# Forgetting attention: mask and key decay added by TensorE, maxima and exponentials taken from the bank

## The chip, the cores and the metric

The kernel runs on one core of one Trainium2 chip. The metric is the device time of one execution in microseconds; of several runs the median is taken. The program covers a whole two-block model plus a mixture-of-experts layer, and the part that is changed is one stage of it, some 45 us long.

## The reference, cut to what matters

All of it is float32, 256 tokens, model width 1024. The second block is "forgetting attention" with 16 heads of 64:

```
log_f = log_sigmoid(f + b_f)                       # one value per token and head
cum   = cumsum(log_f, axis=tokens)                 # per head
for each block of 128 queries (qs .. qe):
    logits = q[qs:qe] @ k[:qe].T + cum[qs:qe, None] - cum[None, :qe]
    p      = softmax(where(query >= key, logits, -inf))
    out    = p @ v[:qe]
```

A softmax over keys doesn't change when a value is added to a whole row, so `cum` of the query (one value for each row) has no effect on `p`; `cum` of the key has.

## The kernel before, in words

Everything is written out by hand: one program for each engine, and semaphores between them. Matmul results go to eight PSUM banks that are handed out in the fixed order of a list (`bank_plan`, line 210 and on for this stage). Each entry of the list names a product and the engine that empties its bank ("A" for ScalarE, "D" for VectorE). `take_bank` on TensorE waits until the bank taken eight entries earlier has been emptied; `bank_filled` counts the filled ones, `emptied["A"]` and `emptied["D"]` count the emptied ones of each engine in the order of the list.

The queries and keys are laid out with the head's 64 values on partitions (`fqT`, `fkT`). A head has two tiles of scores in one bank: queries 0 to 127 against keys 0 to 127 (128 columns), queries 128 to 255 against all keys (256 columns). The stage is a loop over 16 heads, skewed across the engines:

- TensorE, step i (lines 1004 to 1014): the scores of head i (`fox_scores`), the turning of the probabilities of head i-2 (`fox_turn`, three 128x128 transposes, line 991), and in every even step from 4 on the product with the values for a pair of heads (`fox_read`, lines 1001 and 1002). The scores are four float32 matmuls: for each of the two tiles the product of query and key (L982), then a product that adds the key's decay row (L984): a one-hot column of the identity, broadcast, picks the head's row out of `ncumT`.
- VectorE, step i (lines 1846 to 1873): adds the query's decay (`cum`) and the mask to both tiles, bank to SBUF (L1852, L1854; after this the bank is free), takes the negated row maxima from SBUF (L1858, L1859), then for head i-1 the reciprocal of the row sums and the scaling of the probabilities (L1864 to L1866), and in every even step from 4 on the gating of a finished pair (L1871, L1872, L1563).
- ScalarE, step i (lines 1345 to 1356): the two exponentials with row sums (L1348, L1350), then the copy of the turned probabilities of head i-2 out of their bank (L1356).

`logits`, `prob` and `mx` have two buffers. VectorE starts head i after the exponentials of head i-2 are done.

Ahead of the loop TensorE computes the decay sums by six small matmuls into bank `fox_cum` (L965 to L970), and then transposes queries (`fox_qT`) and keys (`fox_kT`) into four banks each (L780). `transpose_in` takes its four banks before its first transpose. In the list stand `fox_cum`, four `fox_qT`, four `fox_kT`: the last bank of the keys is the one that `fox_cum` had, eight entries earlier. VectorE copies `cum` and builds `ncumT` (L1839 to L1841), then copies the keys out (L1843). ScalarE scales the queries (L1340). After the loop comes the output product of the stage (`out_product`, L768 to L770).

SyncE loads weights into a ring of three slots; a slot is loaded again when its old weights have been split into `units` by ScalarE and VectorE. `fp32r` in the rows is the rounded float32 type; large products use it, in three matmuls of high and low parts.

Of the kernel before, what the change touches and what calls it, by code (L numbers as in the profile page):

```python
# [33 lines left out]
F32 = mybir.dt.float32  # L34
I32 = mybir.dt.int32
ACT = mybir.ActivationFunctionType
ALU = mybir.AluOpType
AX = mybir.AxisListType

P = 128  # L40
# [147 lines left out]
def bank_plan():  # L188

    def total(layer, j):  # L190
        return [("mod_sum", SUMS.index((layer, j)), "D")] + ([("mod_sum_high", layer, "D")] if j == GATE else [])

    g = [("c_cols", 0, "A"), ("vecs", 0, "D")] + [("x0T", i, "A") for i in range(4)] + total(0, SCALE) + total(0, SHIFT)
    g += [("ret_q", i, "D") for i in range(RH)]
    g += [("ret_k", i, "D") for i in range(RH)]
    g += [("ret_v", i, "A") for i in range(6)] + total(0, GATE) + [("ret_v", i, "A") for i in range(6, 8)]
    g += [("ret_g", i, "A") for i in range(2)] + total(1, SCALE) + [("ret_g", i, "A") for i in range(2, 4)]
    g += [("ret_s", h, "D") for h in range(2)]
    g += [("ret_g", i, "A") for i in range(4, 6)] + total(1, SHIFT) + [("ret_s", h, "D") for h in range(2, RH)]
    g += [("ret_o", i, "D") for i in range(4)]  # L200
    g += [("ret_g", i, "A") for i in range(6, 8)]
    g += [("ret_o", i, "D") for i in range(4, 8)]
    g += [("ret_uT", i, "S") for i in range(8)]
    g += [("ret_y", i, "D") for i in range(4)]
    g += [("x1T", i, "A") for i in range(4)]
    g += [("fox_q", 0, "D"), ("fox_q", 1, "D"), ("fox_f", 0, "D"), ("fox_q", 2, "D"), ("fox_q", 3, "D")]
    g += total(1, GATE) + [("fox_k", i, "D") for i in range(4)]
    g += [("fox_v", i, "A") for i in range(4)] + [("fox_g", i, "A") for i in range(4)]
    g += [("fox_cum", 0, "D")]
    g += [("fox_qT", i, "A") for i in range(4)] + [("fox_kT", i, "D") for i in range(4)]  # L210
    for i in range(FH + 3):
        if i < FH:
            g += [("fox_s", i, "D")]
        if 2 <= i < FH + 2:
            g += [("fox_pT", i - 2, "A")]
        if i >= 4 and i % 2 == 0:
            g += [("fox_o", (i - 4) // 2, "D")]
    g += [("fox_y", i, "D") for i in range(4)]
    g += [("x2T", i, "S") for i in range(4)]
    for c in range(2):  # L220
        g += [("conf_g", 2 * c + i, "A") for i in range(2)] + [("conf_a", 2 * c + i, "D") for i in range(2)]
    g += [("conf_taps", i, "A") for i in CONV_BY_TENSOR]
    g += [("conf_cT", i, "D") for i in range(4)] + [("conf_nT", i, "A") for i in range(4)]
    g += [("conf_y", i, "D") for i in range(4)]
    g += [("x3T", i, "S") for i in range(4)]
    for c in range(6):
        n = min(2, FB // 2 - 2 * c)
        g += [("ffn_gate", 2 * c + i, "A") for i in range(n)] + [("ffn_up", 2 * c + i, "D") for i in range(n)]
    g += [("ffn_y", i, "D") for i in range(4)]
    g += [("x4T", i, "S") for i in range(4)]  # L230
    for c in range(2):
        g += [("sc_c", 2 * c + i, "A") for i in range(2)] + [("sc_h", 2 * c + i, "D") for i in range(2)]
        g += [("sc_b", 2 * c + i, "D") for i in range(2)]
    g += [("sc_y", i, "D") for i in range(4)]
    g += [("x5T", i, "A") for i in range(4)]
    g += [("route", 0, "D"), ("rank", 0, "D")]
    return g
# [58 lines left out]
def build(nc, t, out):  # L296
# [4 lines left out]
    with ctx:  # L301
        def sb(name, shape, dt=F32):
            return ctx.enter_context(nc.sbuf_tensor(name, shape, dt))
# [10 lines left out]
        xr_at = nc.sbuf_base  # L314
        xr = sb("xr", [P, 2, KB, T], F32R)
        X = nc.alloc_sbuf_tensor_at("X", [P, (KB + 1) * T], F32, offset=xr_at)
        region_at = nc.sbuf_base
        R = nc.alloc_sbuf_tensor_at("R", [P, REGION], F32, offset=region_at)
        H = nc.alloc_sbuf_tensor_at("H", [P, REGION], F32R, offset=region_at)
# [11 lines left out]
        bf_row = sb("bf_row", [P, FH])  # L331
        logf = sb("logf", [P, NT, FH])
        logf_t = sb("logf_t", [P, 2, NT * FH])
        cum = sb("cum", [P, NT, FH])
        mx = sb("mx", [P, 2, 2])
        rsum = sb("rsum", [P, 2, 2])
        rinv = sb("rinv", [P, 2, 2])
# [55 lines left out]
        y_tmp = region(10240, 2, 512)  # L393
        wf = region(7424, KB, FH)

        ncumT = X[:, 0:T]
        xn1 = region(8192, NT, D)
        fq_tok, fk_tok = region(0, NT, D), region(2048, NT, D)
        fv, fgT = region(4096, NT, D), region(6144, KB, T)
# [2 lines left out]
        fqT = [region(8192, KB, T), X[:, T:T + KB * T].rearrange("p (k t) -> p k t", k=KB)]  # L402
        fuT = split_region(0, KB, T)
        fsq = region(12288, 2, 512)
        logits = region(12288, 2, 384)
        prob = region(13056, 2, 384)
        probT = region(13824, 4, 384)

# [83 lines left out]
        logf_mid = sem("logf_mid")  # L492
        logf_ready = sem("logf_ready")
        logits_ready = sem("logits_ready")
        probs_exp = sem("probs_exp")
        probs_ready = sem("probs_ready")
        half_ready = sem("half_ready")
        conv_ready = sem("conv_ready")
# [247 lines left out]
        def _(pe):  # L746
# [215 lines left out]

            pe.wait_ge(logf_ready, 1)
            b = take_bank("fox_cum", 0)
            mm(b[:, 0:FH], tri, logf[:, 0, :], start=True, stop=True)  # L965
            mm(b[:, FH:2 * FH], ones, logf[:, 0, :], start=True, stop=False)
            mm(b[:, FH:2 * FH], tri, logf[:, 1, :], start=False, stop=True)
            mm(b[0:FH, P:2 * P], logf[:, 0, :], tri, start=True, stop=True)
            mm(b[0:FH, 2 * P:3 * P], logf[:, 0, :], ones, start=True, stop=False)
            mm(b[0:FH, 2 * P:3 * P], logf[:, 1, :], tri, start=False, stop=True).then_inc(bank_filled, 1)  # L970
            wait_emptied("fox_q", 3)
            transpose_in("fox_qT", fq_tok)
            wait_emptied("fox_k", 3)
# [2 lines left out]
            def fox_scores(h):  # L976

                b = take_bank("fox_s", h)
                blk = h // 2
                pick = ident[:, h:h + 1].to_broadcast([P, P])  # L980
                for tt, lo, n in ((0, 0, P), (1, P, T)):
                    mm(b[:, lo:lo + n], fqT[h % 2][:, blk, tt * P:(tt + 1) * P], fkT[:, blk, 0:n],  # L982
                       start=True, stop=False)
                    last = mm(b[:, lo:lo + n], pick, ncumT[:, 0:n], start=False, stop=True)  # L984
                last.then_inc(bank_filled, 1)

            def fox_turn(h):
# [205 lines left out]
        def _(act):  # L1193
# [149 lines left out]
            for i in range(FH + 2):  # L1343
                if i < FH:
                    act.wait_ge(logits_ready, i + 1)
                    if i >= 2:
                        act.wait_ge(bank_filled, BANK_AT["fox_pT", i - 2] + 1)
                    nc.scalar.activation(prob[:, i % 2, 0:P], logits[:, i % 2, 0:P], ACT.Exp,  # L1348
                                         bias=mx[:, i % 2, 0:1], accum_out=rsum[:, i % 2, 0:1])
                    nc.scalar.activation(prob[:, i % 2, P:3 * P], logits[:, i % 2, P:3 * P], ACT.Exp,  # L1350
                                         bias=mx[:, i % 2, 1:2], accum_out=rsum[:, i % 2, 1:2]).then_inc(probs_exp, 1)
                if i >= 2:
                    h = i - 2
                    if h >= 4:
                        act.wait_ge(bank_filled, BANK_AT["fox_o", (h - 4) // 2] + 1)
                    nc.scalar.copy(probT[:, h % 4, :], bank("fox_pT", h)[:, 0:3 * P]).then_inc(emptied["A"], 1)  # L1356
# [182 lines left out]
        def _(dve):  # L1539
# [296 lines left out]
            for key in (("fox_v", 0), ("fox_v", 1), ("fox_g", 0)):  # L1836
                lows_until(CHUNK_AT[key] + 2)
            b = bank("fox_cum", 0)
            v.tensor_copy(cum[:, :, :].rearrange("p t h -> p (t h)"), b[:, 0:NT * FH])  # L1839
            step(v.memset(ncumT, 0.0))  # L1840
            v.tensor_scalar(ncumT[0:FH, :], b[0:FH, P:3 * P], -1.0, None, ALU.mult).then_inc(emptied["D"], 1)  # L1841
            for g in range(4):
                v.tensor_copy(fkT[:, 2 * g:2 * g + 2, :], pairs(bank("fox_kT", g))).then_inc(emptied["D"], 1)  # L1843

            wait_emptied("fox_kT", 3)
            for i in range(FH + 3):
                if i < FH:
                    b = bank("fox_s", i)
                    if i >= 2:
                        dve.wait_ge(probs_exp, i - 1)  # L1850
                    j = i % 2
                    v.scalar_tensor_tensor(logits[:, j, 0:P], b[:, 0:P], cum[:, 0, i:i + 1],  # L1852
                                           const[:, C_MASK + P:C_MASK + 2 * P], ALU.add, ALU.add)
                    v.scalar_tensor_tensor(logits[:, j, P:3 * P], b[:, P:3 * P], cum[:, 1, i:i + 1],  # L1854
                                           const[:, C_MASK:C_MASK + 2 * P], ALU.add, ALU.add
                                           ).then_inc(emptied["D"], 1)
                    wait_emptied("fox_s", i)
                    v.tensor_reduce(mx[:, j, 0:1], logits[:, j, 0:P], AX.X, ALU.max, negate=True)  # L1858
                    v.tensor_reduce(mx[:, j, 1:2], logits[:, j, P:3 * P], AX.X, ALU.max, negate=True  # L1859
                                    ).then_inc(logits_ready, 1)  # L1860
                if 1 <= i <= FH:
                    h, j = i - 1, (i - 1) % 2
                    dve.wait_ge(probs_exp, h + 1)
                    step(v.reciprocal(rinv[:, j, :], rsum[:, j, :]))  # L1864
                    v.tensor_scalar(prob[:, j, 0:P], prob[:, j, 0:P], rinv[:, j, 0:1], None, ALU.mult)
                    v.tensor_scalar(prob[:, j, P:3 * P], prob[:, j, P:3 * P], rinv[:, j, 1:2], None, ALU.mult  # L1866
# [370 lines left out]
```

## Time and profile before

| what | value |
| --- | --- |
| median of 3 runs | 1893.32 us (1892.92 to 1893.88) |
| profiled execution, its own time | 1889.13 us |
| span of the profiled execution | 1887.2 us |
| mean granted TensorE clock | 0.973 |
| PE busy | 1747.1 us (93%) |
| DVE busy | 1424.1 us (75%) |
| ACT busy | 1020.0 us (54%) |

How to read it: the span goes from the first to the last instruction; busy time is the sum over an engine's instructions without overlaps. PE is TensorE, PEld its weight loads, DVE VectorE, ACT ScalarE, SP SyncE. A duration contains the time in which the next instruction of the same engine is already in the pipe, so the distance between two starts is often shorter than the duration. A float32 matmul stands as two records ("x2"), an fp32r matmul as one.

### The profile page before, as it was taken

The numbers are of one execution on the slowest core, as the hardware profiler recorded it, in microseconds if no ns is written. First come the engines' busy times: TensorE is split into PE (matmuls) and PEld (weight loads), VectorE is DVE, ScalarE is ACT, GpSimd is POOL, SyncE is SP. The second block draws the span as 40 slices with busy tenths as digits, with TensorE's granted clock in tenths as the row PEclk, the third lists the DMA queues.
The fourth block names the chain that finished last, engine by engine and source line by source line (L and its number), as shares of the span: only waits on it lengthen the run. The fifth ranks groups of instructions, "written<-read, shape, count | busy, mean of one in ns | idle before, by whom it ended". The sixth has DMA issues, their size and how long they took to land.

```text
span 1887.2 us, 23377 instructions
## 1 busy us (share of the span) xinstructions
PE 1747.1 (93%) x9401; PEld 1487.6 (79%) x9401; DVE 1424.1 (75%) x1253; ACT 1020.0 (54%) x804; POOL 52.0 (3%) x42
## 2 busy tenths in 40 slices
PE   2899889988989999797999999999999999999995
PEld 2888678967769998796788887888878888888784
DVE  5686866485865553576787987988979799898896
ACT  1334244454224332332776777767777677677762
POOL 0000002000000000001000000000000000000100
PEclk9999899999999999897999999999999999999998
DMA  9579173604655656453999999999999999999992
GB/s 336 190 288 361 68 256 137 219 3 148 180 182 201 246 195 230 156 179 123 336 361 370 382 372 368 368 371 380 371 374 365 374 387 372 386 382 383 370 379 112
DMA packets 217700, 531.19 MB, mean 281 GB/s; under 512 B 7606, under 2 KB 13902, under 8 KB 217337
## 3 DMA queue, kind: packets, MB, share of 16 engines
q1 hardware_dynamic: 210624, 514.52, 74.8%
q10 hardware_dynamic: 5640, 10.39, 1.5%
q0 software_dynamic: 1328, 4.73, 0.7%
q8 instruction: 82, 1.34, 0.3%
q14 instruction: 26, 0.21, 0.0%
HBM read 521.93 MB, written 16.09 MB: 285 GB/s over the span
## 4 chain that ended last, share of the span: by engine, by line
PE 79%; DVE 9%; DMA 5%; ACT 3%; issue 2%; POOL 1%; ACTq 0%; DVEq 0%; POOLq 0%; SPq 0%
PE psum L768 25%; PE psum L770 25%; PE psum L769 25%; DMA ring<-in_moe_w_gate 3%; DVE units L1563 3%; DMA ring<-in_moe_w_up 1%; ACT units L1445 1%; PE psum L1129 1%; DMA ring<-in_mod_w 1%; POOL root_out L1512 1%; DVE R L1910 1%; DVE stats L1973 1%; DMA R<-in_positions 0%; DVE R L1637 0%; DVE x L1982 0%
## 5 line engine op out<-in xcount | busy, mean ns | idle before, releaser
L1563 DVE TENSOR_TENSOR units<-ring,units 128x2048 fp32r<-128x2048 f32 x451 | 1011.0, 2279 | 271.2 <-ACT units L1243 167.6
L1445 ACT CAST units<-ring 128x2048 fp32r<-128x2048 f32 x332 | 625.5, 1916 | 237.1 <-PE psum L770 69.9
L768 PE MATMUL psum<-units,xr 128*128 128x512 f32 x1120 | 445.2, 397 | 13.4 <-DVE units L1563 6.0
L770 PE MATMUL psum<-units,xr 128*128 128x512 f32 x1120 | 438.9, 392 | 0.0
L769 PE MATMUL psum<-units,xr 128*128 128x512 f32 x1120 | 438.6, 392 | 0.0
L1243 ACT CAST units<-ring 128x2048 fp32r<-128x2048 f32 (+1 forms) x119 | 218.8, 1882 | 219.3 <-PE psum L770 186.3
L768 PE MATMUL psum<-units,H 128*128 128x512 f32 x696 | 274.6, 395 | 2.1 <-DVE H L1563 2.1
L769 PE MATMUL psum<-units,H 128*128 128x512 f32 x696 | 272.4, 391 | 0.0
L770 PE MATMUL psum<-units,H 128*128 128x512 f32 x696 | 272.2, 391 | 0.0
L768 PEld LDWEIGHTS psum<-units,xr 128*128 128x128 f32 x1120 | 211.8, 189 | 61.0 <-issue 9.3
L768 PE MATMUL psum<-xr,units 128*128 128x256 f32 x864 | 247.1, 286 | 12.6 <-DVE units L1563 11.4
L770 PEld LDWEIGHTS psum<-units,xr 128*128 128x128 f32 x1120 | 211.7, 189 | 45.3
L769 PE MATMUL psum<-xr,units 128*128 128x256 f32 x864 | 246.5, 285 | 0.0
L770 PE MATMUL psum<-xr,units 128*128 128x256 f32 x864 | 246.4, 285 | 0.0
L769 PEld LDWEIGHTS psum<-units,xr 128*128 128x128 f32 x1120 | 212.0, 189 | 43.4 <-issue 0.7
L768 PEld LDWEIGHTS psum<-xr,units 128*128 128x128 f32 x864 | 168.1, 195 | 13.6 <-DVE units L1563 11.4
L769 PEld LDWEIGHTS psum<-xr,units 128*128 128x128 f32 x864 | 168.0, 194 | 0.0
L770 PEld LDWEIGHTS psum<-xr,units 128*128 128x128 f32 x864 | 167.9, 194 | 0.0
L768 PEld LDWEIGHTS psum<-units,H 128*128 128x128 f32 x696 | 131.6, 189 | 30.2 <-issue 1.8
L770 PEld LDWEIGHTS psum<-units,H 128*128 128x128 f32 x696 | 131.5, 189 | 27.9
L769 PEld LDWEIGHTS psum<-units,H 128*128 128x128 f32 x696 | 131.7, 189 | 26.9
L2146 DVE TENSOR_TENSOR R<-R,psum 128x512 f32<-128x512 f32 x56 | 38.4, 685 | 33.4 <-PE psum L770 33.4
(260 smaller groups left out, 1022.1 us busy)
## 6 DMA issues: line engine op xcount, KB each, us to landing
ring<-in_moe_w_gate SPq DMA_DIRECT2D x56, 2048.0 KB, 9.7
ring<-in_moe_w_up SPq DMA_DIRECT2D x56, 2048.0 KB, 10.2
ring<-in_moe_w_down SPq DMA_DIRECT2D x56, 2048.0 KB, 9.8
ring<-in_mod_w SPq DMA_DIRECT2D x12, 2048.0 KB, 9.8
ring<-in_ret_w_in SPq DMA_DIRECT2D x11, 2048.0 KB, 9.7
ring<-in_fox_w_in SPq DMA_DIRECT2D x8, 2048.0 KB, 8.9
ring<-in_sc_w_in SPq DMA_DIRECT2D x6, 2048.0 KB, 7.9
ring<-in_ffn_w_gate SPq DMA_DIRECT2D x5, 2048.0 KB, 8.4
```

The lines of the kernel that those rows point to most:

```text
L768: mm(dst, left[0], right[0], start=first, stop=False)
L769: mm(dst, left[0], right[1], start=False, stop=False)
L770: return mm(dst, left[1], right[0], start=False, stop=last)
L1129: last = nc.tensor.transpose(b[:, j * P:(j + 1) * P], e_ht[:, (q * PAIRS + c) % 2, j * P:(j + 1) * P], ident)
L1243: nc.scalar.copy(dst[0], src).then_inc(unit_high, 3 - len(parts))
L1445: nc.scalar.copy(*expert_unit_parts(q, j, half, 0)).then_inc(unit_high, 1)
L1512: nc.gpsimd.tensor_tensor(root_out[:, n % 2, 0:w], root_in[:, n % 2, 0:w], neg_half[:, 0:w], ALU.pow).then_inc(root_ready, 1)
L1563: return v.tensor_tensor(dst, src, high.bitcast(F32), ALU.subtract)
L1910: ins = v.scalar_tensor_tensor(conv[:, i, :], u_pad[:, i, k:k + T], vec[:, i, V_DW + k:V_DW + k + 1], conv[:, i, :], ALU.mult, ALU.add)
L1973: last = v.bn_stats(stats[:, tt, half, :], z[:, tt, hs])
L2146: v.tensor_tensor(e_ht[:, (q * PAIRS + c) % 2, :], e_s[:, (q * PAIRS + c) % 2, :], psum[:, 4 + (q * 2 * PAIRS + 2 * c + 1) % 4, :], ALU.mu ...
```

## The change

The query's decay is no longer added. The mask and the key's decay are both added by TensorE, in fp32r: two matmuls of 384 columns ahead of the two score products take the place of the two float32 decay matmuls. So that nothing of the decay is lost to rounding, it is held as a rounded part (partitions 0 to 15) and the remainder (partitions 32 to 47), and the one-hot column has a one for each. VectorE takes the maxima from the bank, ScalarE the exponentials; the exponentials now empty the bank. The tiles `logits` and `cum` go, and the semaphore `probs_exp` with them: its waits are on the emptied bank now.

```diff
-            g += [("fox_s", i, "D")]
+            g += [("fox_s", i, "A")]
...
-            mm(b[:, 0:FH], tri, logf[:, 0, :], start=True, stop=True)
-            mm(b[:, FH:2 * FH], ones, logf[:, 0, :], start=True, stop=False)
-            mm(b[:, FH:2 * FH], tri, logf[:, 1, :], start=False, stop=True)
-            mm(b[0:FH, P:2 * P], logf[:, 0, :], tri, start=True, stop=True)
-            mm(b[0:FH, 2 * P:3 * P], logf[:, 0, :], ones, start=True, stop=False)
-            mm(b[0:FH, 2 * P:3 * P], logf[:, 1, :], tri, start=False, stop=True).then_inc(bank_filled, 1)
+            for at in (0, QUAD):
+                rows_at = b[at:at + FH]
+                mm(rows_at[:, P:2 * P], logf[:, 0, :], tri, start=True, stop=True)
+                mm(rows_at[:, 2 * P:3 * P], logf[:, 0, :], ones, start=True, stop=False)
+                last = mm(rows_at[:, 2 * P:3 * P], logf[:, 1, :], tri, start=False, stop=True)
+            last.then_inc(bank_filled, 1)
...
-                pick = ident[:, h:h + 1].to_broadcast([P, P])
+                pick = pick_r[:, h:h + 1].to_broadcast([P, P])
+                mm(b[:, 0:3 * P], ident_r, mask_r, start=True, stop=False)
+                mm(b[:, 0:3 * P], pick, ncum, start=False, stop=False)
                 for tt, lo, n in ((0, 0, P), (1, P, T)):
-                    mm(b[:, lo:lo + n], fqT[h % 2][:, blk, tt * P:(tt + 1) * P], fkT[:, blk, 0:n],
-                       start=True, stop=False)
-                    last = mm(b[:, lo:lo + n], pick, ncumT[:, 0:n], start=False, stop=True)
+                    last = mm(b[:, lo:lo + n], fqT[h % 2][:, blk, tt * P:(tt + 1) * P], fkT[:, blk, 0:n],
+                              start=False, stop=(tt == 1))
...
-                    nc.scalar.activation(prob[:, i % 2, 0:P], logits[:, i % 2, 0:P], ACT.Exp,
+                    b = bank("fox_s", i)
+                    nc.scalar.activation(prob[:, i % 2, 0:P], b[:, 0:P], ACT.Exp,
                                          bias=mx[:, i % 2, 0:1], accum_out=rsum[:, i % 2, 0:1])
-                    nc.scalar.activation(prob[:, i % 2, P:3 * P], logits[:, i % 2, P:3 * P], ACT.Exp,
-                                         bias=mx[:, i % 2, 1:2], accum_out=rsum[:, i % 2, 1:2]).then_inc(probs_exp, 1)
+                    nc.scalar.activation(prob[:, i % 2, P:3 * P], b[:, P:3 * P], ACT.Exp,
+                                         bias=mx[:, i % 2, 1:2], accum_out=rsum[:, i % 2, 1:2]).then_inc(emptied["A"], 1)
...
-            v.tensor_copy(cum[:, :, :].rearrange("p t h -> p (t h)"), b[:, 0:NT * FH])
-            step(v.memset(ncumT, 0.0))
-            v.tensor_scalar(ncumT[0:FH, :], b[0:FH, P:3 * P], -1.0, None, ALU.mult).then_inc(emptied["D"], 1)
+            v.tensor_copy(mask_r[:, 0:P], const[:, C_MASK + P:C_MASK + 2 * P])
+            v.tensor_copy(mask_r[:, P:3 * P], const[:, C_MASK:C_MASK + 2 * P])
+            v.tensor_copy(ident_r, ident)
+            v.tensor_tensor(pick_r, ident[:, 0:FH], ident[:, QUAD:QUAD + FH], ALU.add)
+            step(v.memset(ncum.bitcast(F32), 0.0))
+            step(v.tensor_scalar(ncum_high[QUAD:QUAD + FH, :], b[QUAD:QUAD + FH, P:3 * P], -1.0, None, ALU.mult))
+            for lo, n in ((0, P), (P, T)):
+                v.tensor_scalar(ncum[0:FH, lo:lo + n], b[0:FH, P:P + n], -1.0, None, ALU.mult)
+                last = v.scalar_tensor_tensor(ncum[QUAD:QUAD + FH, lo:lo + n], b[QUAD:QUAD + FH, P:P + n], -1.0,
+                                              ncum_high[QUAD:QUAD + FH, 0:n].bitcast(F32), ALU.mult, ALU.subtract)
+            last.then_inc(emptied["D"], 1)
...
-            wait_emptied("fox_kT", 3)
             for i in range(FH + 3):
                 if i < FH:
                     b = bank("fox_s", i)
                     if i >= 2:
-                        dve.wait_ge(probs_exp, i - 1)
+                        wait_emptied("fox_s", i - 2)
                     j = i % 2
-                    v.scalar_tensor_tensor(logits[:, j, 0:P], b[:, 0:P], cum[:, 0, i:i + 1],
-                                           const[:, C_MASK + P:C_MASK + 2 * P], ALU.add, ALU.add)
-                    v.scalar_tensor_tensor(logits[:, j, P:3 * P], b[:, P:3 * P], cum[:, 1, i:i + 1],
-                                           const[:, C_MASK:C_MASK + 2 * P], ALU.add, ALU.add
-                                           ).then_inc(emptied["D"], 1)
-                    wait_emptied("fox_s", i)
-                    v.tensor_reduce(mx[:, j, 0:1], logits[:, j, 0:P], AX.X, ALU.max, negate=True)
-                    v.tensor_reduce(mx[:, j, 1:2], logits[:, j, P:3 * P], AX.X, ALU.max, negate=True
+                    v.tensor_reduce(mx[:, j, 0:1], b[:, 0:P], AX.X, ALU.max, negate=True)
+                    v.tensor_reduce(mx[:, j, 1:2], b[:, P:3 * P], AX.X, ALU.max, negate=True
                                     ).then_inc(logits_ready, 1)
                 if 1 <= i <= FH:
                     h, j = i - 1, (i - 1) % 2
-                    dve.wait_ge(probs_exp, h + 1)
+                    wait_emptied("fox_s", h)
```

The new tiles `ncum`, `ncum_high`, `mask_r`, `ident_r` and `pick_r` lie in the memory of `xr`, which is free in this stage.

## Rows read from the trace of the kernel before

**Rows 1.** Windows view: length; busy of PE, PEld, DVE, ACT, POOL; PEclk; DMA share; GB/s.

```profile
403.36:408.70 5.34, 4.54 (x32) 3.51 (x31) 4.91 (x18) 2.70 (x10) 0.00 (x0) 1.00 0.01 3
```

**Rows 2.** Timeline by engine, the same pair; columns: start, duration, engine, line; idle before.

```profile
403.36 0.35 DVE L1852 SCALAR_TENSOR_TENSOR R<-psum,cum,const 128x128 f32<-128x128 f32 x1 [0.22 <-PE psum L984]
404.13 0.29 DVE L1858 TENSOR_REDUCE mx<-R 128x1 f32<-128x128 f32 x1
...
404.78 0.40 ACT L1348 ACTIVATE R<-R,mx 128x128 f32<-128x128 f32 x1 [2.03 <-DVE mx L1859]
...
406.27 0.66 PE L1001 MATMUL psum<-R 128*64 128x256 f32 x4 [0.21 <-ACT R L1356]
407.08 0.49 PE L982 MATMUL psum<-R,X 128*128 128x128 f32 x2
407.41 0.39 PE L984 MATMUL psum<-X,const 128*128 128x128 f32 x2
407.63 0.60 PE L982 MATMUL psum<-R,X 128*128 128x256 f32 x2
408.06 0.59 PE L984 MATMUL psum<-X,const 128*128 128x256 f32 x2
408.50 0.49 PE L991 MATMUL psum<-const,R 128*128 128x128 f32 x3
...
408.70 0.35 DVE L1852 SCALAR_TENSOR_TENSOR R<-psum,cum,const 128x128 f32<-128x128 f32 x1 [0.22 <-PE psum L984]
```

**Rows 3.** Timeline, TensorE and VectorE at the end of the loop.

```profile
424.37 0.66 PE L1001 MATMUL psum<-R 128*64 128x256 f32 x4 [0.71 <-ACT R L1356]
...
425.29 0.42 DVE L1871 TENSOR_TENSOR R<-psum,R 128x256 f32<-128x256 f32 x1 [0.86 <-PE psum L1002]
...
426.42 2.29 DVE L1563 TENSOR_TENSOR units<-ring,units 128x2048 fp32r<-128x2048 f32 x1
```

**Rows 4.** Groups by line and shape: reads of PSUM beside reads of SBUF.

```profile
L1563 DVE TENSOR_TENSOR H<-R,H 128x256 fp32r<-128x256 f32 x8 | 3.4, 425 | 0.3
L1871 DVE TENSOR_TENSOR R<-psum,R 128x256 f32<-128x256 f32 x8 | 3.4, 419 | 1.5 <-PE psum L1002 1.5
L1350 ACT ACTIVATE R<-R,mx 128x256 f32<-128x256 f32 x16 | 7.9, 495 | 0.0
L1372 ACT ACTIVATE R<-psum,vec 128x256 f32<-128x256 f32 x6 | 2.9, 475 | 21.5 <-PE psum L1030 21.5
```

**Rows 5.** Chain of waits: one fp32r matmul of 512 and one of 256 columns.

```profile
425.91 0.23 PE psum L770
...
456.03 0.12 PE psum L769
```

**Rows 6.** Timeline, ahead of the loop and its first heads, three engines.

```profile
376.14 3.71 PE L780 MATMUL psum<-const,R 128*128 128x128 f32 x32
376.25 0.19 DVE L1839 COPY cum<-psum 128x32 f32<-128x32 f32 x1 [5.94 <-PE psum L970]
376.44 0.27 DVE L1840 MEMSET X<- 128x256 f32 x1
376.75 0.41 DVE L1841 TENSOR_SCALAR X<-psum 16x256 f32<-16x256 f32 x1
379.24 2.48 DVE L1843 COPY R<-psum 128x512 f32<-128x512 f32 x4 [2.08 <-PE psum L780]
...
382.25 1.28 ACT L1348 ACT_TABLE_LOAD   x1
...
385.82 0.39 PE L982 MATMUL psum<-R,X 128*128 128x128 f32 x2
...
388.76 0.40 ACT L1348 ACTIVATE R<-R,mx 128x128 f32<-128x128 f32 x1 [0.76 <-DVE mx L1859]
```

**Rows 7.** Waits of the load queue from 360 to 440 us; columns: total, times, longest.

```profile
SPq L678 <- DVE units L1563: 71.3, 2, 60.2
```

**Rows 8.** Windows view, a stretch with a lower granted clock.

```profile
220.00:240.00 20.00, 17.26 (x65) 14.03 (x66) 19.68 (x21) 1.65 (x3) 0.00 (x0) 0.76 0.38 126
```

More of the change, by code:

```diff
@@ L316, in build @@
         X = nc.alloc_sbuf_tensor_at("X", [P, (KB + 1) * T], F32, offset=xr_at)
+        Xr = nc.alloc_sbuf_tensor_at("Xr", [P, 2 * KB * T], F32R, offset=xr_at)
         region_at = nc.sbuf_base
@@ L333, in build @@
         logf_t = sb("logf_t", [P, 2, NT * FH])
-        cum = sb("cum", [P, NT, FH])
         mx = sb("mx", [P, 2, 2])
@@ L394, in build @@
         wf = region(7424, KB, FH)
-        ncumT = X[:, 0:T]
+        ncum = Xr[:, KB * T + T:KB * T + T + 3 * P]
+        ncum_high = Xr[:, KB * T + T + 3 * P:KB * T + T + 3 * P + T]
+        mask_r = Xr[:, 3072:3072 + 3 * P]
+        ident_r = Xr[:, 3456:3456 + P]
+        pick_r = Xr[:, 3584:3584 + FH]
         xn1 = region(8192, NT, D)
@@ L404, in build @@
         fsq = region(12288, 2, 512)
-        logits = region(12288, 2, 384)
         prob = region(13056, 2, 384)
@@ L494, in build @@
         logits_ready = sem("logits_ready")
-        probs_exp = sem("probs_exp")
         probs_ready = sem("probs_ready")
```

## The prediction

> **What bounds the kernel now.** I read the page first (its slices show TensorE nearly always busy and the load engines silent in one slice only, that of the attention loop), then the windows over that loop, the chain of waits through it, the timeline of each engine over one pair of heads, and the groups by shape for the prices. The reader is to see that this stage, unlike most others, is not held by any one engine's work. A pair of heads takes 5.34 us, in which TensorE is busy 4.54, VectorE 4.91 and ScalarE 2.70 [rows 1]. What repeats is a ring of waits through all three [rows 2]: VectorE adds and reduces, from 403.36 to the exponential at 404.78, 1.42; exponentials and copy of the turned probabilities until TensorE reads them at 406.27, 1.49; that product until the next scores start at 407.08, 0.81; scores until VectorE starts at 408.70, 1.62. The sum is 5.34, the whole period. So what the change cuts from this ring counts in full, once for each pair, until another ring takes over.
>
> **The scores (L982, L984).** Removed: two float32 decay matmuls, 408.06 to 408.50 and 407.41 to 407.63, 0.44 + 0.22 = 0.66 [rows 2]. Added: two fp32r matmuls of 384 columns. 256 columns take 0.12, 512 take 0.23 [rows 5], so one takes between these; I take the middle, 0.175, so 0.35 for both (0.24 to 0.46). Net -0.31 a head; a ring has one head's scores in it. Scores after a read go from 1.62 to 1.31.
>
> **VectorE in the loop.** L1852 and L1854 go, and with them the wait for their own end: from 403.36 to the first maximum at 404.13, 0.77 a head [rows 2]. The maxima read PSUM instead of SBUF. No row has a reduction from PSUM; the nearest pair is the tensor_tensor, 419 ns from PSUM against 425 from SBUF [rows 4], so I take no difference; the two maxima until the exponential stay at 404.13 to 404.78, 0.65. Ceiling: that they take as long as the two removed passes over the same columns, 0.77, or 0.12 more; the other end is a gain of 0.01.
>
> **ScalarE in the loop.** Same instructions, from PSUM. With a per-partition operand, 256 columns take 475 ns from PSUM and 495 from SBUF [rows 4] (the latter writes row sums too). I take 0; from 0.04 less to 0.04 more a head.
> On these two the Trainium skill speaks against half of the change: "VectorE: DVE Perf Modes", section on the TRN2 errata, gives VectorE 58 fixed cycles from SBUF and 120 from PSUM, and ScalarE 224 and 172. By that, as an estimate, two maxima cost 0.13 more and two exponentials 0.09 less, 0.04 more a ring, about 0.3 in all; the VectorE rows above don't show the difference.
>
> **New period.** 0.65 + 1.49 + 0.81 + 1.31 = 4.26, so 1.08 less. What is late next: the route from the read over the gating of the finished pair: read at 424.37 to the gate at 425.29, 0.92, gate to the next instruction at 426.42, 1.13 [rows 3], then 0.65 + 1.49: 4.19. Just below 4.26, so it hides, but more savings on TensorE would be lost to it. By work, TensorE would be busy 4.54 - 0.62 = 3.92, VectorE 4.91 - 1.54 = 3.37 [rows 1], so neither is the bound. VectorE's second head of the pair and its waits for the exponentials of the head before fit: they end at most 0.65 + 1.49 after its maxima began, and the scaling of that head comes only after the other head's scaling and maxima. The bank of head i is freed by the exponentials instead of the first passes, some 2 us later; it is wanted three heads on, over 6 us later: nothing.
>
> **Ahead of the loop.** TensorE: three 128-wide small matmuls out, three more 16-wide in, all of a kind with the transposes, 3.71 over 32 = 0.116 a record [rows 6]; 0, within 0.2.
> VectorE: before, three instructions, 376.25 to about 377.16 [rows 6]. Now ten, all behind the wait for the `fox_cum` bank: mask copies, identity and pick about 0.8, memset of 384 columns with its wait 0.45 (256 take 0.31 from start to start), the rounded row 0.46 with its wait (0.41 for the like), then 0.3 + 0.4 + 0.45 + 0.5 for the four that fill `ncum`: 3.3 in all (2.0 if each takes 0.2, 4.6 if each takes 0.46). They end at 379.55.
> Who waits: `transpose_in` for the keys takes its four banks first, and the last of them is `fox_cum`'s. Before, that bank was free at 377.16 and the query transposes ended at 376.14 + 16 x 0.116 = 378.00, so it cost nothing. Now the key transposes start at 379.6, 1.6 late (0.3 to 2.9), so key copies start at 379.24 + 1.6 = 380.84, take 2.48, and the first maxima are done at 383.32 + 0.65 = 383.97. The cover is ScalarE's table load, 382.25 to 383.53, behind which the first exponential stood anyway. What sticks out is 0.44 (0 to 1.75).
>
> **The sum.** Through the first heads: the scores of head 3 start at 385.82 [rows 6], behind the turn of head 0, which follows from exponential 0, so now at 386.26. Behind a turn they took 0.1 less than behind a read (first distance 0.22 instead of 0.33), so 1.21 now: maxima at 387.47, exponential 3 at 388.12 instead of 388.76 [rows 6]: 0.64 won. From there to exponential 15 are six rings (scores of heads 5, 7, ... 15): 6 x 1.08 = 6.48. The tail behind exponential 15 (read of pair 6, turn 15, copy, read of pair 7) has no changed length. Won at the start of the output product: 7.1 us.
>
> **Behind the loop.** The load queue sleeps through the stage: it waits 71.3 us for VectorE's split of weights, 60.2 in one piece [rows 7], the DMA share in the loop is 0.01 [rows 1]. The ring is full before the loop starts, so nothing that runs on its own clock is overtaken; loads, splits and products move forward together. The saving should reach the end whole.
> The profiled execution took 1889.13 us (span 1887.2), so 1882.0 by its own measure. The median of the runs shown is 4.2 above it; the difference is applied to that: 1893.3 - 7.1 = 1886.2.
>
> **Rivals.**
> Smaller gain: reductions from PSUM at their ceiling (6 x 0.12 = 0.7), fp32r matmuls at 0.23 each (6 x 0.11 = 0.7) and the setup at its own (1.3) leave 4.4: 1888.9. For it: no row shows these forms. Against it: each nearest row is better. 0.14.
> The mask product isn't cheap: an fp32r matmul joined to float32 ones in one accumulation runs at their rate. 384 columns are then 0.44 x 1.5 = 0.66 each, two of them 1.3 instead of 0.66: period 5.22 rather than 5.34, and 6 x 0.12 is about what the setup loses: 1893, no change. Against it: rate goes with an instruction's own type in all rows. 0.04.
> The gain doesn't travel: some later stage starts at a time set by loads. Then 1893.3. For it: the expert layer keeps the DMA engines full. Against it: rows 7; its loads too start only when slots come free. 0.06.
> Slower: the chip grants TensorE the lower of its two levels, 1.2 instead of 2.4 GHz, in this loop. It is 1.00 there now [rows 1], and 0.76 in a stretch where the engine is busy by the record 17.26 of 20 us [rows 8], so a fall is possible at such shares. Then the 3.92 us of matmuls in a pair become some 7.2 and TensorE itself the bound: 1.9 more than now for each of 7 pairs, +13, 1906. From about a third of the loop at the lower level on, the gain is eaten. Against it: the same products in less time, 3.92 of 4.26, a busier engine than 4.54 of 5.34. The Trainium skill ("TensorE: Matmul & The Clock Gate", "What's actually happening") says that activity releases the throttle, which speaks against this rival as well. 0.04.
>
> **Chances and range.** Forecast 0.72, the rest as above. What this kernel's measurement tells from no change is 0.2%, 3.8 us. Faster 0.72 + 0.14 = 0.86; within 0.2% 0.10; slower 0.04. The low end takes the good bounds (no setup cost, 0.12 matmuls: 8.3 won, and half a us for the runs), 1884.4; the high end takes the smaller gain whole and 0.6 for the runs, 1889.5. That leaves out 0.14 for the other three rivals and a little at each end.
>
> **What would show it.** Right: VectorE's maxima of odd heads 4.26 apart; the first key copy at about 380.8 instead of 379.24; the first exponential at about 384.0; the key transposes in a group of their own, waiting for VectorE; the last read of a pair at about 417.3 instead of 424.37; the stretches behind it unchanged in length. Wrong: a period above 4.6, a reduction from PSUM above 0.5 us, a granted clock below 1.00 in the loop, or a longer idle of TensorE for loads further on.

## The result, and the profile after

| | before | changed |
| --- | --- | --- |
| first timing, median of 7 | 1893.32 us | 1881.79 us |
| ratio, 95% interval | | 0.9947 (0.9936 to 0.9958) |
| profiled execution, span | 1889.13, 1887.2 us | 1882.47, 1880.7 us |

The kernel is faster, and by more than was forecast: the median lies 2.6 us below the range. Two later timings of the same kernel gave 0.9966 (0.9950 to 0.9982) and 0.9959 (0.9943 to 0.9974). Read the profile first for the part that was changed.

One pair of heads in the loop, in the windows view (length; busy PE, PEld, DVE, ACT, POOL; clock; DMA), the answer to [rows 1]:

```profile
402.61:406.81 4.20, 3.93 (x28) 3.00 (x27) 3.62 (x14) 2.57 (x10) 0.00 (x0) 1.00 0.01 4
```

And the ring of waits in the timeline, the answer to [rows 2] and to the gating of [rows 3]:

```profile
404.70 0.66 PE L1004 MATMUL psum<-R 128*64 128x256 f32 x4
405.50 0.44 PE L983 MATMUL psum<-Xr 128*128 128x384 f32 x1
405.78 0.34 PE L984 MATMUL psum<-Xr 128*128 128x384 f32 x1
405.96 0.82 PE L986 MATMUL psum<-R,X 128*128 128x128 f32 x4
406.61 0.49 PE L994 MATMUL psum<-const,R 128*128 128x128 f32 x3
...
405.61 0.42 DVE L1876 TENSOR_TENSOR R<-psum,R 128x256 f32<-128x256 f32 x1 [0.39 <-PE psum L1005]
406.07 0.29 DVE L1877 CAST H<-R 128x256 fp32r<-128x256 f32 x1
406.40 0.43 DVE L1567 TENSOR_TENSOR H<-R,H 128x256 fp32r<-128x256 f32 x1
406.81 0.29 DVE L1863 TENSOR_REDUCE mx<-psum 128x1 f32<-128x128 f32 x1
...
407.47 0.37 ACT L1352 ACTIVATE R<-psum,mx 128x128 f32<-128x128 f32 x1 [1.54 <-DVE mx L1864]
...
408.90 0.66 PE L1004 MATMUL psum<-R 128*64 128x256 f32 x4
```

The period is 4.20 instead of 5.34. "Read" is the product with the values for a pair of heads (L1004 here). Two routes lead from the read at 404.70 to the maxima at 406.81, and they arrive together. On one, the scores end when the next turn (L994) starts, 406.61, and some 0.2 later VectorE could go on. On the other, the gating starts at 405.61 and holds VectorE for 1.20. Then the maxima take 0.66, and exponentials and copy 1.43 until the next read at 408.90.

The groups by shape, the answer to [rows 4]: maxima from SBUF in the kernel before, then maxima and exponentials from PSUM in the changed one.

```profile
L1859 DVE TENSOR_REDUCE mx<-R 128x1 f32<-128x256 f32 x16 | 6.5, 409 | 0.0
...
L1864 DVE TENSOR_REDUCE mx<-psum 128x1 f32<-128x256 f32 x16 | 6.6, 413 | 0.0
L1354 ACT ACTIVATE R<-psum,mx 128x256 f32<-128x256 f32 x16 | 7.4, 466 | 0.0
```

Ahead of the loop, the answer to [rows 6]: the transposes stand in two groups now, and the keys' wait for VectorE's setup.

```profile
374.44 1.97 PE L782 MATMUL psum<-const,R 128*128 128x128 f32 x16
377.67 1.94 PE L782 MATMUL psum<-const,R 128*128 128x128 f32 x16 [1.26 <-DVE Xr L1851]
...
374.55 0.23 DVE L1843 CAST Xr<-const 128x128 fp32r<-128x128 f32 x1 [5.60 <-PE psum L971]
...
377.11 0.42 DVE L1851 SCALAR_TENSOR_TENSOR Xr<-psum,Xr 16x256 fp32r<-16x256 f32 x1
378.99 2.48 DVE L1855 COPY R<-psum 128x512 f32<-128x512 f32 x4 [1.47 <-PE psum L782]
...
381.11 1.28 ACT L1352 ACT_TABLE_LOAD   x1 [0.57 <-PE psum L986]
...
386.46 0.37 ACT L1352 ACTIVATE R<-psum,mx 128x128 f32<-128x128 f32 x1 [0.32 <-DVE mx L1864]
```

The end of the loop:

```profile
415.17 0.66 PE L1004 MATMUL psum<-R 128*64 128x256 f32 x4 [0.71 <-ACT R L1360]
```

S is the length of the stage from the first query transpose to this last read. It is 415.17 - 374.44 = 40.73; before, 424.37 - 376.14 = 48.23 [rows 3, 6]. So the change took 7.5 us out of the stage. The first timing shows 11.5. The experiments ask what the ring of waits is made of, and where the other 4 us are.

### The profile page after: what moved, and what is told of

It is laid out like the page before. It is cut to its first block, busy times and chain, and to the rows that moved or that the text cites. A ratio compares the mean times of both kernels' runs of the same rounds, so it can differ in the third digit from the quotient of the medians.

```text
span 1880.7 us, 23289 instructions
## 1 busy us (share of the span) xinstructions
PE 1739.5 (92%) x9369; PEld 1481.5 (79%) x9369; DVE 1414.6 (75%) x1228; ACT 1017.5 (54%) x804; POOL 51.4 (3%) x42
## 4 chain that ended last, share of the span: by engine, by line
PE 66%; DVE 6%; DMA 3%; issue 2%; ACT 2%; POOL 1%; SPq 0%; POOLq 0%; DVEq 0%; ACTq 0%
PE psum L770 21%; PE psum L772 20%; PE psum L771 20%; DVE units L1567 2%; DMA ring<-in_moe_w_gate 1%; PE psum L1132 1%; DMA ring<-in_moe_w_up 1%; ACT units L1449 1%; POOL root_out L1516 1%; DVE stats L1978 1%; DVE x L1987 0%; DVE R L1915 0%; PE psum L986 0%; DMA u_rows<-R 0%; DVE R L1975 0%
```

## The experiments

**Is the further gain the change's?** The changed kernel again, the changed kernel with the unused tile `cum` put back, the kernel before with `cum` moved behind the other small tiles, and later the changed kernel once more.

> The changed kernel once more. S is the stage from the first query transpose to the last read of a pair: 48.2 us before, 40.7 after the change. Theory R (the ring is all of it): S is again 40.7 and the kernel is 7.5 us faster than before within the spread of the runs; the further 4 us of the first timing were spread. Theory L (the removed tile moved every small tile behind it by 128 bytes, and that brought more): 11 to 12 us faster again. Theory D (later stages run faster because they come at another time): 11 to 12 again as well, and a stage behind the loop is shorter in this profile too.

> The changed kernel with the unused tile cum still allocated, so that all tiles behind it lie where they lay before. Theory L: 4 us of the gain are lost, about 1886. Theories R and D: as the repeat of the changed kernel beside it, within 1 us.

```diff
+        cum = sb("cum", [P, NT, FH])
         mx = sb("mx", [P, 2, 2])
```

> The kernel before with cum allocated last, so that the tiles behind it lie as in the changed kernel. Theory L: 4 us faster than before. Theories R and D: no change, S 48.2.

```diff
-        cum = sb("cum", [P, NT, FH])
...
         gate_back = sb("gate_back", [P, 2, NT])
+        cum = sb("cum", [P, NT, FH])
```

> The changed kernel a third time, in the same rounds as the version beside it. By the ring alone S is 40.7 again and the time 7.5 us below before. If the first timing (11.5 below) was the true size, it is 11 to 12 below; in this profile the length of the expert layer, 986 to 995 us in the profiles so far, decides where its own time falls, not S.

Measured: the repeat 0.9966, the padded one 0.9960 (0.9942 to 0.9978), the moved `cum` 1.0007 (0.9995 to 1.0019), the last repeat 0.9959. The layout (theory L) falls: neither kernel moved by 4 us. What these timings did show is how far runs of one kernel lie apart: 34 runs of before span 1885.05 to 1897.85, twelve of the changed kernel 1876.12 to 1892.11.

Every kernel's profile can be cut into four stretches: up to the first query transpose; S; from there to VectorE's last step for the router (`back`, L2105 of before); and from there to its last write of `x` (L1982), the expert layer. Each line below comes from one execution. Its own time is some 6 us more than the sum, for what stands behind the last stretch and outside the span.

```
              before stage    S       to router's end   experts  own time
before            376.14    48.23         468.7         989.8    1889.13
before_moved      375.03    48.54         470.9         993.3    1893.96
after             374.44    40.73         468.6         992.5    1882.47
again             375.59    40.71         470.2         992.7    1885.42
pad               374.48    40.75         468.9         993.0    1883.24
again2            375.90    40.72         469.9         996.1    1888.76
f32               375.60    51.19         468.6         995.0    1896.57
passback          375.69    45.66         468.9         987.3    1883.68
ahead             375.74    41.20         468.4         991.1    1882.59
later             375.09    41.00         468.5         989.5    1880.34
both              374.19    39.75         469.8         987.8    1877.65
early             375.36    40.17         470.2         985.8    1877.66
best              375.52    39.21         471.3         989.0    1881.13
best2             374.15    38.39         470.9         996.5    1886.17
```

The code outside S is the same in all. S repeats within 0.04 us for the four with the changed loop; the expert layer lies between 985.8 and 996.5. In the profile of before the DMA engines are busy 0.98 of it:

```profile
893.10:1882.90 989.80, 960.98 (x4342) 792.18 (x4341) 837.32 (x475) 702.66 (x466) 20.90 (x10) 0.99 0.98 361
```

Theory D (later stages shorten because they start at another time) falls too, as far as these profiles go. In the four with the changed loop the stretch up to the router was 0.1 us shorter in one and 0.2 to 1.5 longer in the others than in the one profile of before, and the expert layer was 2.7, 2.9, 3.2 and 6.3 longer. The one execution of the first timing that was profiled shows the same: its time is 6.7 us below the profiled one of before, made of 1.7 ahead of the stage, 7.5 in S, 0.1 behind it, and 2.7 lost in the expert layer.

So the gain that the change has is S. That the first timing's further 4 us are spread is what the later timings show: in the first, the median of before was 1893.32 and later 1890.95 to 1892.12, the changed kernel's was 1881.79 and later 1884.63 and 1884.74. Both medians of the first timing lay on the side that widens the gap. The interval of the first ratio (8.0 to 12.1 us) leaves 7.5 out; the three later timings of the changed loop, weighted by their runs, give 7.3 by their medians, and all four 8. Which stretch was short in the first seven runs isn't known, because only one of them has a profile.

The mean granted clock of the whole run does not account for the spread. In 17 of the 34 runs of before it was 0.963 to 0.969, in 17 it was 0.970 to 0.975. The first took 1892.3 on average and the second 1889.9, but each group alone spans some 9 us, and in the twelve runs of the changed kernel beside them the group with the lower clock was the faster (1883.4 against 1885.4).

A smaller source of spread stands in the profile of the moved `cum`: the granted clock fell around the end of the loop, 0.76 in 424 to 434. In the ten us behind the last read the thirteen other profiles have 1.00. The output product's matmuls started 0.43 apart instead of 0.23.

```profile
424.00:434.00 10.00, 10.00 (x40) 7.81 (x37) 5.55 (x5) 4.37 (x3) 0.00 (x0) 0.76 0.17 44
...
425.65 0.63 PE L769 MATMUL psum<-units,H 128*128 128x512 f32 x1
426.08 0.63 PE L770 MATMUL psum<-units,H 128*128 128x512 f32 x1
```

It fell behind a stretch in which TensorE waits for scaling and copies of the last heads, busy 6.38 of 10 us (414 to 424, clock 0.90 on average). The profile of before has the same 6.38 in its last ten us of the loop and kept 1.00. From the last read to the router's end before_moved took 470.9 instead of 468.7, so the fall cost some 2 us (an estimate). So the clock rival was not empty: in one profile of fourteen, with the old loop, the clock fell where the loop ends.

A second place shows in all fourteen. Between 20 and 40 us behind the last read the granted clock is 0.91 in the seven profiles whose stretch to the router's end is 468.4 to 468.9, and in before_moved. It is 0.74 or 0.83 in the six that took 469.8 to 471.3. The code there is the same in all, and up to 3 us come and go together with the clock; that is seen side by side and was not tested.

**The parts of the change.** First VectorE's and ScalarE's part without the cheap matmuls, then TensorE's part without theirs.

> The changed kernel with the mask and decay products in float32 instead of fp32r, same values. One float32 product of 384 columns should take 0.65, so scores take 0.96 more, the ring of waits 5.15 instead of 4.20. Theory R: S is 47 (seven heads' scores on the way times 0.96), time within 1 us of before, so the gain of the whole change hangs on the rounded type. Theory D: as S is back at its old length, the later stages are too, and the time is that of before. Theory L: 4 us faster than before all the same.

```diff
-                pick = pick_r[:, h:h + 1].to_broadcast([P, P])
-                mm(b[:, 0:3 * P], ident_r, mask_r, start=True, stop=False)
-                mm(b[:, 0:3 * P], pick, ncum, start=False, stop=False)
+                pick = pick_r[:, h:h + 1].bitcast(F32).to_broadcast([P, P])
+                mm(b[:, 0:3 * P], ident_r.bitcast(F32), mask_r.bitcast(F32), start=True, stop=False)
+                mm(b[:, 0:3 * P], pick, ncum.bitcast(F32), start=False, stop=False)
```

Measured: 1.0016 (1.0003 to 1.0028), slower than before, S 51.19 where 47 was expected. The price of one product was right, what bounds the loop was not:

```profile
403.73 0.91 PE L983 MATMUL psum<-Xr 128*128 128x384 f32 x2
404.48 0.81 PE L984 MATMUL psum<-Xr 128*128 128x384 f32 x2
405.13 0.82 PE L986 MATMUL psum<-R,X 128*128 128x128 f32 x4
...
408.06 0.49 PE L994 MATMUL psum<-const,R 128*128 128x128 f32 x3
408.48 0.66 PE L1004 MATMUL psum<-R 128*64 128x256 f32 x4
...
409.28 0.91 PE L983 MATMUL psum<-Xr 128*128 128x384 f32 x2
```

From L984 to L986 it is the expected 0.65. But both heads of a pair pay it, and TensorE runs through without a gap: 409.28 - 403.73 = 5.55, where the ring alone would have given 5.15. So this run is no clean measure of VectorE's and ScalarE's part; it shows that the rounded type is what makes the move to TensorE pay. In float32 the change loses 3 us (S 51.19 against 48.23) instead of winning 7.5.

> The changed kernel, with VectorE's pass from bank to SBUF put back as a plain copy of both tiles; maxima and exponentials read SBUF again. It keeps the mask, the decay and the rounded products on TensorE, so it is TensorE's part of the change alone. Theory R (the ring): 0.77 more in each ring and once at head 3, S 40.7 + 7 x 0.7 = 45.6 to 46.1. Rival (most of the gain came from the shorter scores): S below 43.

```diff
+        logits = region(12288, 2, 384)
...
+                    v.tensor_scalar(logits[:, j, 0:P], b[:, 0:P], 0.0, None, ALU.add)
+                    step(v.tensor_scalar(logits[:, j, P:3 * P], b[:, P:3 * P], 0.0, None, ALU.add))
-                    v.tensor_reduce(mx[:, j, 0:1], b[:, 0:P], AX.X, ALU.max, negate=True)
-                    v.tensor_reduce(mx[:, j, 1:2], b[:, P:3 * P], AX.X, ALU.max, negate=True
+                    v.tensor_reduce(mx[:, j, 0:1], logits[:, j, 0:P], AX.X, ALU.max, negate=True)
+                    v.tensor_reduce(mx[:, j, 1:2], logits[:, j, P:3 * P], AX.X, ALU.max, negate=True
```

The exponentials kept reading the bank here, unlike what the expectation says. Measured: 0.9996 (0.9979 to 1.0013), S 45.66. VectorE's pass put back costs 4.93 of the 7.5. The whole time agrees with a rest of 2.6 us, and doesn't tell it from none. The copies hold VectorE 0.66 before the maxima start:

```profile
402.01 0.29 DVE L1864 TENSOR_SCALAR R<-psum 128x128 f32<-128x128 f32 x1
402.22 0.41 DVE L1865 TENSOR_SCALAR R<-psum 128x256 f32<-128x256 f32 x1
402.67 0.29 DVE L1866 TENSOR_REDUCE mx<-R 128x1 f32<-128x128 f32 x1
```

The next such copy starts at 406.87, so the period is 4.86, the ring of 4.20 and these 0.66. VectorE has no idle time in it: here its own work is as long as the ring.

**Which route closes the ring?**

> The changed kernel, with the mask and decay products of odd heads issued ahead of the read of a pair instead of behind it, so that they stand in the time in which TensorE waits for ScalarE's copy. Theory T (two routes of nearly equal length close the ring of 4.20 us: one over the scores, one over VectorE's gating of the finished pair): nothing, S stays within 0.3 of 40.7. Theory P (the scores alone close it): the ring loses 0.43, six times, S 38.1.

`fox_decay` is the first part of `fox_scores`, now a function of its own: it takes the bank and issues the mask and the decay product.

```diff
+                    if i < 5 or i % 2 == 0:
+                        fox_decay(i)
                     fox_scores(i)
...
+                if i >= 4 and i % 2 == 0 and i + 1 < FH:
+                    fox_decay(i + 1)
                 if i >= 4 and i % 2 == 0:
                     fox_read((i - 4) // 2)
```

> The changed kernel, with VectorE's gating of a pair moved behind the next odd head's maxima and scaling. Theory T: nothing, S within 0.3 of 40.7, because the scores then close the ring at 4.19. Theory G (the gating alone closes it): the ring falls to below 4, S below 39.5.

```diff
-                if i >= 4 and i % 2 == 0:
-                    g = (i - 4) // 2
+                if i >= 5 and i % 2 == (1 if i < FH else 0):
+                    g = (i - 5) // 2 if i < FH else (i - 4) // 2
```

> Both moves together. Theory T: the ring falls from 4.20 to 0.80 + 0.88 + 0.66 + 1.43 = 3.77, S is 40.7 - 6 x 0.43 = 38.1. Theories P and G: no more than the one move that works alone.

Measured S: 41.20 and 41.00 for one move alone, against 40.7, and 39.75 for both. The times can't tell these kernels from the changed one: 0.9958 (0.9931 to 0.9986), 0.9954 (0.9928 to 0.9979) and 0.9961 (0.9942 to 0.9979). The rows show each time the other route closing the ring. With the early products, the scores end at 403.73, and VectorE starts the maxima only behind the gating, at 404.23, without idle time. With the later gating, it waits for the scores:

```profile
403.73 0.49 PE L998 MATMUL psum<-const,R 128*128 128x128 f32 x3
...
403.89 0.43 DVE L1575 TENSOR_TENSOR H<-R,H 128x256 fp32r<-128x256 f32 x1
404.23 0.28 DVE L1871 TENSOR_REDUCE mx<-psum 128x1 f32<-128x128 f32 x1
```

```profile
403.06 0.49 PE L994 MATMUL psum<-const,R 128*128 128x128 f32 x3
...
403.26 0.29 DVE L1863 TENSOR_REDUCE mx<-psum 128x1 f32<-128x128 f32 x1 [0.62 <-PE psum L986]
```

So neither the scores nor the gating closes the ring alone, and taking both away opens it: theory T holds, P and G fall. But the two together gave 1.0, not 2.6. The ring, read to read, is 3.99:

```profile
399.75 0.66 PE L1008 MATMUL psum<-R 128*64 128x256 f32 x4
...
400.56 0.92 PE L990 MATMUL psum<-R,X 128*128 128x128 f32 x4
...
402.94 0.52 PE L998 MATMUL psum<-const,R 128*128 128x128 f32 x3
403.21 0.42 PE L982 MATMUL psum<-Xr 128*128 128x384 f32 x1
403.47 0.34 PE L983 MATMUL psum<-Xr 128*128 128x384 f32 x1
403.74 0.66 PE L1008 MATMUL psum<-R 128*64 128x256 f32 x4
```

The products that were to stand in TensorE's idle time stand right in front of the read, behind a turn that itself waits for VectorE. From the exponential at 402.17 to the read it is 1.57 instead of 1.43. The last experiment puts them ahead of that turn. The early products alone have the same flaw, a ring of 4.28; without it they would have had some 4.15 (an estimate), still no more than 0.05 won.

**The setup, and a version that joins the steps.**

> The changed kernel, with the four copies of mask, identity and pick made ahead of the wait for the decay sums, in the idle VectorE (memory of the old logits tile). They take 0.67 of the 2.95 us that the key transposes wait for. Theory W (the key transposes wait for VectorE's setup and this reaches the first exponential): key transposes 0.67 earlier, S 40.1. Rival (the table load covers it, as the prediction had it for the old kernel): S 40.7.

```diff
-        mask_r = Xr[:, 3072:3072 + 3 * P]
+        mask_r = H[:, 12288:12288 + 3 * P]
...
-            b = bank("fox_cum", 0)
             v.tensor_copy(mask_r[:, 0:P], const[:, C_MASK + P:C_MASK + 2 * P])
...
             v.tensor_tensor(pick_r, ident[:, 0:FH], ident[:, QUAD:QUAD + FH], ALU.add)
+            b = bank("fox_cum", 0)
```

Measured: S 40.17, 0.56 less; the key transposes start 2.66 behind the query ones instead of 3.23, so theory W holds. Time 0.9953 (0.9937 to 0.9968).

> Both moves of the loop and the early copies together. Theories T and W: S 40.7 - 2.6 - 0.6 = 37.5, time 3 us below the changed kernel, 10.7 below the kernel before. Rival (a third ring, over the turn of the even head or ScalarE's copies, takes over): S above 38.5.

Measured: S 39.21, which is the sum of the two parts (1.0 + 0.6), but above the 38.5 from which on the expectation speaks for its rival; 0.9957 (0.9941 to 0.9974). Whether a third ring took over or the placing of the products in front of the read held it is what the next kernel tells.

> As the best one, but the early mask and decay products of odd heads stand ahead of the turn of the even head instead of behind it. In both moves together they ended at 403.64 in front of a read that could have started at about 403.6, and the ring was 3.99 instead of 3.77. Theory T (what kept the ring at 3.99 is that they stood in front of the read): the ring falls to about 3.85, S 39.2 - 6 x 0.14 = 38.4. Rival (TensorE and VectorE are full in that ring, and the order makes no difference): S 39.2. The time should be 9 to 10 us below the kernel before, 2 below the changed kernel, which the spread of the runs may hide.

The edit against the version before it:

```diff
+                if i >= 4 and i % 2 == 0 and i + 1 < FH:
+                    fox_decay(i + 1)
                 if 2 <= i < FH + 2:
                     fox_turn(i - 2)
-                if i >= 4 and i % 2 == 0 and i + 1 < FH:
-                    fox_decay(i + 1)
```

Measured: S 38.39, as expected, the ring 3.86 (398.62 to 402.48):

```profile
398.62 0.66 PE L1008 MATMUL psum<-R 128*64 128x256 f32 x4
...
401.45 0.52 PE L982 MATMUL psum<-H 128*128 128x384 f32 x1
401.81 0.34 PE L983 MATMUL psum<-Xr,H 128*128 128x384 f32 x1
401.99 0.49 PE L998 MATMUL psum<-const,R 128*128 128x128 f32 x3
402.48 0.66 PE L1008 MATMUL psum<-R 128*64 128x256 f32 x4
```

So the placing cost 0.13 of the 0.22 that the ring of 3.99 had over the expected 3.77. The other 0.09 stay: behind a read the first product takes 0.1 more. That product is a float32 one now, and scores until maxima take 0.96 instead of 0.88.

Its time was 0.9943 (0.9924 to 0.9962), the best ratio of all, beside 0.9959 for the changed kernel timed with it. By S it is 2.3 us better than the changed kernel and 9.8 better than before; the intervals overlap, so the timing confirms it against the kernel before only.

## Why the prediction was wrong

**The step that failed is the width for the runs.** The forecast allowed "half a us for the runs" at the low end and 0.6 at the high end, and took 1893.3 as its base; the three runs of before that it had lay within 1 us of each other. The spread of this kernel is over ten: 1885 to 1898 in 34 runs. The twelve runs of the changed kernel beside them have a standard deviation of 4.1, from which the median of seven is uncertain by some 1.9 us (an estimate), so 0.5 was too little by a factor of four. The first timing fell 2.6 us outside the range, the two repeats (1884.63 and 1884.74) inside it. Numbers at hand spoke against the width: the profiled execution of before lay 4.2 below the median, and the prediction itself calls 3.8 us the least that this measurement tells from no change. The mechanism was right and its size was 0.4 off. The low end is also 0.1 too low by its own terms (1893.3 - 8.3 - 0.5 = 1884.5), which changes nothing.

**The period.** Forecast 4.26, measured 4.20. The scores after a read took 1.31 (405.50 to 406.81), as forecast; the two fp32r products of 384 columns 0.28 and 0.18, of which 0.1 is the same surcharge behind a read that [rows 2] has in its first distance, so 0.36 against 0.35. Maxima from PSUM 0.66 against 0.65. Exponentials and copy took 1.43 against 1.49: the one term that was off, 0.06 in each of six rings. VectorE's busy time in a pair came to 3.62 instead of 3.37, TensorE's to 3.93 against 3.92; neither is the bound.

**PSUM as a source.** The taken value was no difference for either engine. VectorE agrees: 413 ns against 409 from SBUF for 256 columns (and 290 against 286 for 128). ScalarE doesn't: 466 ns against 495 [rows 4] for 256 columns, 29 less. By the cycles in the Trainium skill, "VectorE: DVE Perf Modes", section on the TRN2 errata, it would be, as an estimate, 43 ns less for ScalarE and 65 ns more for VectorE. The trace agrees with the first in sign, at two thirds of the size, and shows 4 ns in place of the second.

**The next route.** Gating was put at 4.19 and came to 4.20; it now closes the ring together with the scores. The two single moves show it, since neither helped alone.

**Ahead of the loop.** VectorE's setup took 2.98 (374.55 to 377.53) against 3.3; the key transposes started 3.23 behind the query ones instead of 1.86, 1.4 late against 1.6. The first exponential came 7.96 behind the first transpose instead of 7.39 (376.14 to the end of the table load, [rows 6]), 0.57 against the forecast 0.44. That the two are near each other is in part luck, for the route is another. The forecast had the late maxima stick out over the table load. In the trace the first maxima were done at about 382.04, which alone makes 0.21. Not foreseen: the table load itself no longer started right behind the scaling of the queries, it waited 0.57 for the first scores (its row above). The wait on the filled bank in front of ScalarE's first exponential is new in the changed kernel. At exponential 3 the sum was 0.60 won (12.02 against 12.62), forecast 0.64.

**The sum.** 0.60 + 6 x 1.14 = 7.4, and S says 7.5; forecast 7.1.

**Behind the loop.** Everything moved forward together as forecast, up to the router's end in the first profile: 468.6 against 468.7. In the expert layer the profiles can't show it to 3 us, because it varies by ten.

**The rivals.** The smaller gain did not come: none of its three costs did. A mixed accumulation does not slow the fp32r products; one that is float32 costs 0.65, shown by the float32 kernel. The clock stayed at 1.00 in the new loop (3.93 of 4.20 us busy). The price of that rival, 3.92 us of matmuls becoming some 7.2, stands without its working in the prediction; the 0.43 against 0.23 at the loop's end of the moved `cum` would make it 7.3.

## What to carry to other kernels

Where a stage is a ring of waits through several engines, add up the ring and its nearest rival route, not the work of the engines: what is cut counts in full until the next route is as long, and then only cutting both helps. When a small stage is changed in a long kernel, measure that stage in the profile: it repeated within 0.04 us, where the whole time moved by ten between runs, and take the width of a range from many runs, or from the stage that varies most, not from three runs that agree. Work moved to an engine's idle time has to stand where that engine really waits; one place too late and it delays the one instruction that everyone waits for.

## What was unexpected of the hardware

The expert layer, with its DMA engines busy 0.98, took 985.8 to 996.5 us in fourteen executions of the same code. What makes it vary stays open; no experiment here was aimed at it. Its granted clock was 0.98 or 0.99 in all fourteen. The granted clock fell at the end of the attention loop in one profile and not in the thirteen others, though what TensorE did there before was the same in the profile of before. The load of ScalarE's table started 0.57 us later once its exponential waited for a filled bank.
